# Rotating the causal heads by DMA within SBUF, and moving one mean behind half of a unit

## The reference, cut to what matters

```python
def apply_rope(x, cos, sin):
    half = x.shape[-1] // 2
    x1, x2 = xf[..., :half], xf[..., half:]
    return jnp.concatenate([x1 * c - x2 * s, x2 * c + x1 * s], axis=-1)

q = apply_rope(rmsnorm(q.reshape(b, S, H, 2, D), q_norm_w), cos, sin)
k = apply_rope(rmsnorm(k.reshape(b, S, H, 2, D), k_norm_w), cos, sin)
...
mu = jnp.mean(xf, axis=-1, keepdims=True)
var = jnp.mean(jnp.square(xf - mu), axis=-1, keepdims=True)
```

## Time and profile before

| | |
|---|---|
| median of 3 runs | 3334.14 us |
| the profiled execution's own time | 3338.97 us |
| its span, first to last instruction | 3337.5 us |
| TensorE, busy | 3083.0 us, 92% |
| VectorE, busy | 1850.7 us, 55% |
| ACT, busy | 961.7 us, 29% |
| POOL, busy | 1910.0 us, 57% |
| mean granted TensorE clock | 0.965 |

### The profile page before, as it was taken

How to read it: one execution, slowest core, us unless ns; L and a number is a source line. 1 busy time by engine, 2 the same in 40 slices (tenths; PEclk the granted TensorE clock), 3 DMA queues, 4 the chain that set the end, 5 groups by cost and what they waited for, 6 DMA issues and landing times.

```text
span 3337.5 us, 39578 instructions
## 1 busy us (share of the span) xinstructions
PE 3083.0 (92%) x15146; PEld 2396.7 (72%) x15146; DVE 1850.7 (55%) x2681; ACT 961.7 (29%) x1563; POOL 1910.0 (57%) x1860
## 2 busy tenths in 40 slices
PE   8899989989999999998998999997889998898997
PEld 5687767768778877776876777776677776686675
DVE  6754876741384478676128433335788888512313
ACT  5334213430223421344012323233433333301102
POOL 5565656547676655655667555554556555375451
PEclk9899999999999999999999999999999999999997
DMA  5232222133222222122422222221112121222221
GB/s 195 83 106 103 78 74 76 64 108 137 102 101 102 95 83 88 63 76 89 142 100 96 79 78 79 78 74 60 64 64 76 64 76 64 97 103 88 71 94 59
DMA packets 61069, 294.55 MB, mean 88 GB/s; under 512 B 5680, under 2 KB 10672, under 8 KB 31440
## 3 DMA queue, kind: packets, MB, share of 16 engines
q1 hardware_dynamic: 36384, 247.48, 21.2%
q10 hardware_dynamic: 24496, 44.54, 3.9%
HBM read 274.10 MB, written 16.84 MB: 87 GB/s over the span
## 4 chain that ended last, share of the span: by engine, by line
PE 62%; DVE 27%; ACT 5%; issue 2%; POOL 2%; DMA 1%; DVEq 0%; ACTq 0%; POOLq 0%
PE bank L396 53%; DVE bank L1942 5%; DVE h_lo L1681 2%; DVE rec_cum L2240 1%; DVE rec_ex L2283 1%; POOL w_lo L2464 1%; DVE rec_small L2269 1%; PE bank L735 1%; PE bank L752 1%; PE bank L744 1%; PE bank L924 1%; DVE last_z L2412 1%; DVE bank L1752 1%; POOL w_hi L2462 1%; DVE newton L1660 1%
## 5 line engine op out<-in xcount | busy, mean ns | idle before, releaser
L396 PE MATMUL bank<-h_hi,w_lo 128*128 128x512 f32 x3712 | 1523.2, 410 | 86.9 <-DVE h_lo L1681 32.8
L396 PE MATMUL bank<-h_hi,w_hi 128*128 128x512 f32 x3712 | 1468.8, 396 | 0.0
L396 PE MATMUL bank<-h_lo,w_hi 128*128 128x512 f32 x3712 | 1467.8, 395 | 0.0
L2462 POOL TENSOR_SCALAR w_hi<-w_raw 128x512 fp32r<-128x512 f32 x928 | 673.5, 726 | 1288.7 <-PE bank L396 1224.4
L2464 POOL TENSOR_TENSOR w_lo<-w_raw,w_hi 128x512 fp32r<-128x512 f32 x928 | 1259.6, 1357 | 77.4
L396 PEld LDWEIGHTS bank<-h_hi,w_lo 128*128 128x128 f32 x3712 | 711.2, 192 | 313.5 <-issue 54.6
L396 PEld LDWEIGHTS bank<-h_hi,w_hi 128*128 128x128 f32 x3712 | 709.7, 191 | 155.1
L396 PEld LDWEIGHTS bank<-h_lo,w_hi 128*128 128x128 f32 x3712 | 711.6, 192 | 151.4 <-issue 12.5
L965 ACT ACTIVATE raw<-bank 128x512 f32<-128x512 f32 x148 | 88.6, 598 | 390.3 <-PE bank L396 362.4
L1942 DVE SCALAR_TENSOR_TENSOR bank<-cfm_up,par,bank 128x512 f32<-128x512 f32 x232 | 175.4, 756 | 8.3
L2100 DVE TENSOR_TENSOR xT<-bank,xT 128x512 f32<-128x512 f32 x32 | 22.1, 692 | 221.7 <-PE bank L396 221.0
(11 more groups left out here) (336 smaller groups left out, 2876.7 us busy)
## 6 DMA issues: line engine op xcount, KB each, us to landing
w_raw<-in_wall SPq DMA_DIRECT2D x230, 1024.0 KB, 4.9
x_scratch<-xT ACTq DMA_DIRECT2D x12, 1024.0 KB, 4.7
xT<-x_scratch ACTq DMA_DIRECT2D x12, 1024.0 KB, 6.8
ssd_abc<-acs_scratch ACTq DMA_DIRECT2D x16, 512.0 KB, 3.7
first_xin<-in_x SPq DMA_DIRECT2D x4, 1024.0 KB, 11.6
out<-last_rows ACTq DMA_DIRECT2D x4, 1024.0 KB, 4.3
w_raw<-in_wall SPq DMA_DIRECT2D x8, 256.0 KB, 10.6
raw<-in_wpp ACTq DMA_DIRECT2D x16, 128.0 KB, 2.5
```

Of the source, the lines that this page charges most:

```text
L396: mm = t.matmul(bank[BANK[u]][:, :], w[:, CS16[k]], h[:, k, :], start=(k == 0 and w is m.w_lo[b]), stop=(k == KT - 1 and w is m.w_hi[b] an ...
L2462: g.tensor_scalar(m.w_hi[b][:, part], m.w_raw[b][:, part], 1.0, 1.0, ALU.mult, ALU.mult).then_inc(*s.hi.inc(u, n))
```

## The change

`rot` leaves the constants, and `sin` carries the sign instead. The 16 rotation products (4 heads, queries and keys, 2 layers) leave TensorE's order. ACT issues four DMAs of 32 rows (64 KB) for each of them, from `att_uq` or `att_uk` into `att_tq` or `att_tk`, each row of which is 2 KB. VectorE's product with `sin` now reads `att_tq` or `att_tk` in SBUF instead of a PSUM bank and waits for the four DMAs. For head 0 the swaps stand behind the first of ACT's four squares of the conformer stage, for the others behind ACT's square of the head's output and ahead of its Ln and Exp. The variance's mean moves from the middle of unit `cz 3` to the middle of the next unit, `v 0`, and ACT copies out `cz 3` ahead of its wait for that mean. The transposes of the values wait for the means of q and k instead of the product with `sin`.

```diff
--- before.py
+++ after.py
@@ -48,7 +48,7 @@
     ("dt_bias", 1), ("a_log", 1), ("lq", 2), ("lk", 2), ("lam_init", 1), ("one_minus", 1)])
 PAR2, NPAR2 = _columns([("g_pre", KT), ("g_post", KT), ("g_ple", KT), ("g_hg", 1), ("lbf", 16), ("lbb", 16)])
 CON, NCON = _columns([("ident", P), ("ones", P), ("tri", P), ("pick", SSD_H)])
-CON1, NCON1 = _columns([("blk", P), ("rot", P), ("cos", T), ("sin", T), ("causal", T)])
+CON1, NCON1 = _columns([("blk", P), ("cos", T), ("sin", T), ("causal", T)])
 CON2, NCON2 = _columns([("band", 896), ("inv", 1)])
 NLEV = 6 * 4 * 32
 LEVELS = (16, 8, 4, 2, 1, 0)
@@ -316,7 +316,7 @@
         self.qk = [[t(f"r{n}{b}") for n in "qk"] for b in range(2)]
         self.tq, self.uq = [t(f"t{n}") for n in "qk"], [t(f"u{n}") for n in "qk"]
         self.lam = m.lam
-        self.blk, self.rot = (cols(m.con1, CON1, n, P) for n in ("blk", "rot"))
+        self.blk = cols(m.con1, CON1, "blk", P)
         self.cos, self.sin, self.causal = (cols(m.con1, CON1, n, T) for n in ("cos", "sin", "causal"))
         assert m.at <= SBUF_END - 4 * NCON1
 
@@ -564,14 +564,12 @@
             mm = t.matmul(bank[2][:, :], m.ones, q.uc[:, c, :], start=(c == 0), stop=(c == NT - 1))
         mm.then_inc(*pe.inc("mu", l))
         unit(("cz", l, 2))
-        unit(("cz", l, 3), 0, 2)
-        rotate(l, 0, 0)
+        unit(("cz", l, 3))
+        unit(("v", l, 0), 0, 2)
         t.wait_ge(*dve.at("var", l, NT - 1))
         mean_square("cfm", l)
         leave("att", l)
-        unit(("cz", l, 3), 1, 2)
-        rotate(l, 0, 1)
-        unit(("v", l, 0))
+        unit(("v", l, 0), 1, 2)
         unit(("q", l, 1))
         values_in(l, 0)
 
@@ -591,15 +589,9 @@
         t.wait_ge(*act.at("sq", l, h, n))
         t.matmul(own_bank(h)[:, :], q.blk, q.tq[n][:, :], start=True, stop=True).then_inc(*pe.inc("blk", l, h, n))
 
-    def rotate(l, h, n):
-        q = m.att
-        t.wait_ge(*(dve.at("sin", l, h, 0) if n else dve.at("ms", "qk", l, h, 1)))
-        t.wait_ge(*dve.at("unit", l, h, n))
-        t.matmul(own_bank(h)[:, :], q.rot, q.uq[n][:, :], start=True, stop=True).then_inc(*pe.inc("rot", l, h, n))
-
     def values_in(l, h):
         t.wait_ge(*act.at("evac", UNIT["v", l, h]))
-        t.wait_ge(*dve.at("sin", l, h, 1))
+        t.wait_ge(*dve.at("ms", "qk", l, h, 1))
         for c in range(NC):
             mm = t.transpose(own_bank(h)[:, CS[c]], m.raw[2][:, CS[c]], m.ident)
         mm.then_inc(*pe.inc("vt", l, h))
@@ -674,10 +666,7 @@
             values(h, 3)
             quarters(us, 9, 10)
             finish(h)
-            rotate(l, h + 1, 0)
-            quarters(us, 10, 11)
-            rotate(l, h + 1, 1)
-            quarters(us, 11, 12)
+            quarters(us, 10, 12)
             values_in(l, h + 1)
         us = att_after(l, 3)
         scores(3, 0)
@@ -1186,12 +1175,15 @@
             a.wait_ge(*(dve.at("var", l, c - 1) if c else dve.at("centred", l)))
             a.wait_ge(*act.now())
             a.activation(q.th[:, :], q.uc[:, c, :], ACT.Square).then_inc(*act.inc("csq", l, c))
+            if c == 0:
+                swap(l, 0, 0)
+                swap(l, 0, 1)
+        evac(("cz", l, 3), q.zt[:, 3, :])
         a.wait_ge(*dve.at("ms", "cfm", l))
         a.wait_ge(*act.now())
         a.activation(q.rs[:, :], q.tmp[:, :], ACT.Ln).then_inc(*act.inc())
         a.wait_ge(*act.now())
         a.activation(q.rs[:, :], q.rs[:, :], ACT.Exp, scale=-0.5).then_inc(*act.inc("rs", "cfm", l))
-        evac(("cz", l, 3), q.zt[:, 3, :])
         a.wait_ge(*act.now())
         a.activation(flat(q.th4[:, :, :]), flat(q.zt[:, :, :]), ACT.Tanh, scale=0.5).then_inc(*act.inc("zth", l))
         a.wait_ge(*dve.at("gz", l))
@@ -1222,6 +1214,13 @@
         for n in range(2):
             a.wait_ge(*act.now())
             a.activation(q.tq[n][:, :], q.tq[n][:, :], ACT.Exp, scale=-0.5).then_inc(*act.inc("rs", "qk", l, h, n))
+
+    def swap(l, h, n):
+        q = m.att
+        a.wait_ge(*dve.at("unit", l, h, n))
+        for at in (0, 64):
+            for dst, src in ((at, at + 32), (at + 32, at)):
+                a.dma_start(q.tq[n][dst:dst + 32, :], q.uq[n][src:src + 32, :]).then_inc(*s.half[n].inc("att", l, h))
 
     def attention(l):
         q = m.att
@@ -1281,6 +1280,8 @@
             evac(u1, m.raw[2])
             turn(h, 3)
             output(h)
+            swap(l, h + 1, 0)
+            swap(l, h + 1, 1)
             rstd(q.t0[:, :], q.t1[:, :], "att", l, h)
             a.wait_ge(*dve.at("unit", l, h + 1, 0))
             evac(u2, m.raw[0] if h < 2 else m.raw[3])
@@ -1993,9 +1994,9 @@
     def rope(l, h, n):
         q = m.att
         v.wait_ge(*s.con1.at("con1"))
-        v.wait_ge(*pe.at("rot", l, h, n))
-        v.wait_ge(*dve.now())
-        v.tensor_tensor(q.tq[n][:, :], bank[2 if h else 5][:, :], q.sin, ALU.mult).then_inc(*dve.inc("sin", l, h, n))
+        v.wait_ge(*s.half[n].at("att", l, h))
+        v.wait_ge(*dve.now())
+        v.tensor_tensor(q.tq[n][:, :], q.tq[n][:, :], q.sin, ALU.mult).then_inc(*dve.inc())
         v.wait_ge(*dve.now())
         v.tensor_tensor(q.uq[n][:, :], q.uq[n][:, :], q.cos, ALU.mult).then_inc(*dve.inc())
         v.wait_ge(*dve.now())
@@ -2513,10 +2514,7 @@
     i = np.arange(P)
 
     blk = ((i[:, None] // 64) == (i[None, :] // 64)).astype(f) / f(64)
-    rot = np.zeros((P, P), f)
-    for m in range(P):
-        r = m % 64
-        rot[m + 32 if r < 32 else m - 32, m] = -1.0 if r < 32 else 1.0
+    sign = np.where(i % 64 < 32, -1.0, 1.0).astype(f)[:, None]
     inv = (f(1.0) / (f(10000.0) ** (np.arange(0, 64, 2, dtype=f) / f(64)))).astype(f)
     ang = (np.arange(T, dtype=f)[None, :] * inv[(i % 32)][:, None]).astype(f)
     causal = np.zeros((P, T), f)
@@ -2524,7 +2522,7 @@
     tri = (i[:, None] <= i[None, :]).astype(f)
     pick = (i[:, None] % 32 == np.arange(SSD_H)[None, :]).astype(f)
     con = np.concatenate([eye, np.ones((P, P), f), tri, pick], 1)
-    con1 = np.concatenate([blk, rot, np.cos(ang), np.sin(ang), causal], 1)
+    con1 = np.concatenate([blk, np.cos(ang), sign * np.sin(ang), causal], 1)
 
     diff = np.arange(896)[None, :] - 384 - i[:, None]
     count = np.zeros(diff.shape, np.int64)
```

## The result

The changed kernel takes **3365.07 us**, the median of 4 runs (3364.86 to 3369.43); the kernel before took 3336.23 us beside it (4 runs, 3333.97 to 3340.61). The ratio is 1.0088, with a 95% interval of 1.007 to 1.0105: slower by 29 us. I had forecast 3346 us, slower by 12, with a range up to 3356. The direction was right and the size was not.

What follows compares the result with a forecast made beforehand. The chain of waits was 62% TensorE and 27% VectorE, with VectorE's chain ending each head turn. Terms +9.6 (turns) + 5 (clock) - 2.6 (head 0 and mean) made +12 us: 3346 us, range 3326 to 3356.

Steps and rivals of the forecast that it cites:

- the landing of the keys' swap: At a head turn, VectorE goes on 4.0 us after the keys are ready, at about 612.4: +0.45 us.
- Rival 3: At turns, the keys' swap queues behind SP's 1 MB load, landing 2 us later: 12 more, 3358 us; chance 0.1.
- the clock: Behind new TensorE idles at the six turns, 1.2 GHz instead of 2.4: +5 us, with 0 and 9.6 as ends.
- The estimate of 2.15 us for the last 64 KB: Skill's DMA formula for the swap's last DMA: lands 2.15 us after its issue at 610.3, at 612.5.
- my +12: Whole kernel: the forecast sum, +9.6 + 5 - 2.6 us, slower than the kernel before.
- VectorE's longer chain: At six head turns, VectorE's chain grows 2.5 us, of which 1.9 or 1.0 counts: +9.6 us in all.
- `finish`: At a head turn, VectorE's four operations beside POOL take 5.1 us instead of 4.3: +0.8 us.
- POOL beside the keys' rotation: At a head turn, POOL starts earlier; two operations behind the keys' sine product take 1.0 and 1.6 us: +1.2 us.
- The queries' sine product: Reading two SBUF tiles beside POOL's last operation, it takes 1.6 us instead of 0.69; a turn's sum stays the same.
- Hidden work: At a head turn, ACT's Exp ends at about 614.85 instead of 611.65, hidden by later VectorE; without cover 0.7 us.
- idles at both scores: At a head turn, TensorE waits about 2.5 us for the keys at the first scores, then again for the masks.
- Head 0 and the mean: In each layer's conformer stage, a gain of 1.3 us, -2.6 together; mean's wait vanishes, first scores' wait grows.

Runs made afterwards that it cites:

- run 1: The change, with SP's weights load at each head turn held until the keys' swap has landed, against the kernel before: 3339.49 us, ratio 1.0004.
- run 4: The change with the keys' turn DMAs on SP's queue ahead of its load: first kernel behind SP's wait for POOL, 3358.17 us; second ahead of it, 3341.57 us.
- Run 6: Kernel before with the moved mean, rotations by product, and ACT issuing eight unread swap-sized DMAs a turn: 3339.92 us, ratio 1.0007.
- Run 2: Parts of the change on the kernel before: head 0's swaps with moved mean 3338.00 us; moved mean alone 3331.38; swaps of heads 1 to 3 alone 3364.77.

## Why the prediction was wrong in size

**The step that failed** is the landing of the keys' swap: "I take 3.7 to 4.3 us until VectorE can go on, and 4.0 for the sum", hence "+0.45 us". Without a load ahead of its last DMA, as in runs 1 and 4, the swap of the keys needs 3.9 to 4.0 us, so the number was right for a quiet queue. In the change it was 7.3 to 7.5 us, 3.3 to 3.5 more, at all six turns, and run 1 shows what this cost: 28 us by the ratios, 24.8 in the traces of the turns (309.79 against 284.96). Rival 3 named the mechanism, with 2 us instead of 3.3 and a chance of 0.1. Its sum was wrong too: with 3.9 us of delay at four turns, 3.0 at the last heads and 1.6 each for the clock its terms make 31.2 us in place of the forecast's 14.6, which is 16.6 more and not 12, and so 3363. What I held against it was that the last layer's swap "began during such a load and took no longer". That was no test. The DMA view of before in the four microseconds 1898 to 1902, one by one, with the row of 1899 to 1900 left out (the load again, at 89.2%), is:

```profile
q1 hardware_dynamic: 52, 0.43, 100.5%
...
q10 hardware_dynamic: 29, 0.03, 17.6%
...
q10 hardware_dynamic: 19, 0.02, 9.4%
```

The load filled the engines up to 1900 and ended there, and the first packets of a swap begin about 1 us behind its issue (614.0 for 613.01 in the change), here 1899.8 at the earliest. Not one packet of that swap moved while the load did. The collision itself could be read ahead of time: the trace of before has SP's load issued behind POOL's last operation, which ended at 610.11 (this row takes in the next load too, which stands behind a long wait):

```profile
610.14 13.91 SPq L2496 DMA_DIRECT2D w_raw<-in_wall  x2
```

And the fourth DMA of a swap that starts behind the keys' unit, at 608.35, is issued 3 x 0.65 later, at 610.3. In the change the two stand the same way, 1.86 us from the unit's end to POOL's.

The estimate of 2.15 us for the last 64 KB, which the prediction took from the Trainium skill (DMA: Bandwidth & Descriptors, Anatomy of one DMA), stands there as a fit for DMAs that GpSimd issues. For one that SP issues, the first kernel of run 4 agrees with it: its fourth DMA is issued from about 615.14 on, and VectorE goes on at 617.26, 2.1 us later. In the change the same step took 5.5 us (614.84 to 620.37).

**The rest of the sum was too high.** That my +12 and six times 3.3 us, which make 32, come near the 29 measured is luck. Run 1 is the kernel that the forecast had in mind, with the swap landing after 4.0 us, and it is 1.3 us slower than before (-2 to +5), not 12. At its six turns the traces have 2.3 us where I had +9.6 for VectorE's longer chain, and 4.4 where I had +5 for the clock. The second scores there start 12.45 us behind the end of the keys' unit (610.02 to 622.47), 1.42 later than before instead of 2.5: 0.29 for the swap, 0.29 for the two operations behind the keys' sine product, where I had put 1.2, and 0.84 for `finish`, where I had put 0.8. The step that was too dear is thus POOL beside the keys' rotation: POOL began at 614.78, and of the two operations only the second was longer (0.69 and 0.98 us). Even of the 1.42 us only 0.4 are left in the periods of layer 1; what takes up the rest no run takes apart.

**VectorE's chain in the change**, at the turn shown, has the lengths of the forecast. From the keys' sine product to the end of the rotation it is 3.37 us (620.37 to 623.74) instead of 2.14, +1.23 for the forecast +1.2; from the first `newton` to the end of L2040 5.13 instead of 4.47, +0.66 for +0.8. With +3.70 for the swap that makes 5.6 of the 5.8 us by which the second scores are later behind the end of the keys' unit (16.83, from 612.97 to 629.80, instead of 11.03). The queries' sine product took 1.47 us beside POOL's last operation, and 0.69 when it read a PSUM bank. That is the contention of two SBUF inputs that the Trainium skill names (SBUF — State Buffer, Who interferes with whom). I had said that it would cost nothing at a turn, since the keys' product would come while POOL stood idle. For the queries and in run 1 that held. In the change the late landing put the keys' product beside POOL at four of the six turns, where it took 1.67 to 1.77 us instead of 0.69:

```profile
567.33 1.77 DVE L1999 TENSOR_TENSOR att_tk<-att_tk,con 128x512 f32<-128x512 f32 x1 [3.59 <-DMA att_tk<-att_uk]
```

At these four the rotation is 2.2 to 2.3 us longer than before, and `finish` 0.3 shorter.

**Hidden work.** ACT's Exp ended 6.4 us behind the keys' unit instead of 3.4, as forecast (+3.2), and stayed hidden. Run 6 shows a price of about 1.3 us a turn without that cover (0.6 to 2.0; forecast 0.7).

**TensorE and the clock.** I expected idles at both scores. In the change only the first is there, 5.7 to 6.9 us, and behind it the clock is down, as the windows of TensorE at the turn shown have it (length, busy, granted clock):

```profile
623.00:624.00 1.00, 0.20 (x2) 0.50 0.00 0
624.00:626.00 2.00, 2.00 (x8) 0.50 0.00 0
...
628.00:629.00 1.00, 1.00 (x4) 0.50 0.81 98
...
630.00:631.00 1.00, 1.00 (x6) 1.00 0.93 393
```

At 0.50, which is 1.2 GHz, the quarter of a unit between the two scores takes 6.0 us from score to score instead of 4.29 (5.0 to 6.2 at the six turns), about as long as VectorE's `finish` and the masks: the slow stretch fills the second idle, and so costs almost nothing at this turn by this reading of the rows; no run tests it. The +5 us for the clock were therefore not where I put them. In run 1 the idles are shorter, and at the first two turns of layer 0 the clock falls behind the second one; the two periods that begin there are 2.8 and 1.6 us longer than the 47.65 of layer 1.

**Head 0 and the mean** were forecast at -1.3 us a layer. The wait ahead of the mean vanished and the one ahead of the first scores grew, as written; VectorE took the mean at 495.11, between the 494.3 and 497.6 that I gave. Run 2 gives the parts of this stretch: a gain of 4.3 us for the mean and a loss of 2.25 for the swaps. The net is near my 1.3, though in the time of the whole kernel it can't be seen (1.0000, 0.999 to 1.0009), and I didn't see that the one part was worth having alone.

## What to carry to other kernels

A small DMA that someone waits for must be priced by what else is about to be issued on the other queues, not by its duration in a quiet moment; list for each such DMA the next large transfer and what releases it. Where a large load can get ahead, put the small DMAs first on the load's own queue or hold the load, and mind that everything behind an engine's in-order wait is late too. A change of several parts is best taken apart: here one part gained 0.16% and the other lost 0.85%, and the gaining one never needed the other.

## What the runs showed of the hardware beyond what I expected

A DMA of 64 KB whose issue on ACT's queue ended 0.26 us behind that of a 1 MB load on SP's queue moved its packets only from 619.0 on, when the load was nearly through, though three of the same queue just ahead of it had all passed by 616.0. At the other five turns the order of the issues and the wait were the same (3.44 to 3.68 us). The same load, issued 0.05 us behind four such DMAs on their own queue (613.60 behind 613.55), did not hold them up. At this size the second queue's turn came behind nearly the whole of the load and not in shares with it; what in the DMA's path made it so, and whether it holds for other sizes, no run here shows. Issuing one such DMA took ACT 0.51 to 0.66 us, 0.61 in the median, and SP 0.60.
